# A hybrid retention / DeltaNet trunk on one core: waits for each bank apart, a weight split moved ahead of a root, small joins placed among q products, and the columns of q made at another place

## The reference, cut to what matters

```
proj = h @ w_in                                   # q | k | v | z | beta | a
q, k, v = silu(causal depthwise conv of q|k|v)
q = l2norm(q) * d**-0.5 ; k = l2norm(k)           # the norms are columns: one number per head and token
lower = strict part of (k b) k^T * decay           # 64-token chunks in the reference; tiles of 128 in the kernel
a_mat = eye + lower ; sol = triangular_solve(a_mat, [v b, k b exp(g)])
qk = q k^T * decay
scan over chunks: v_new = u - w S ; out = q_dec S + qk v_new ; S = S exp(g_last) + k_dec^T v_new
o = rmsnorm(out) * silu(z) ; out = o @ w_out
```

## Time and profile before

| | |
|---|---|
| three timed runs | 1481.12, 1483.14, 1483.98 us; median 1483.14 |
| the profiled execution | 1481.87 us, of which 1480.1 us are the span of the trace |
| TensorE busy | 1453.2 us, 98% of the span |
| TensorE weight loads | 1220.5 us, 82% |
| VectorE, ScalarE, GpSimd busy | 591.6 (40%), 546.0 (37%), 655.5 us (44%) |
| mean granted TensorE clock | 0.993 of full |
| TensorE on the chain that ended last | 90% of the span |

### The profile page before, as it was taken

How to read it: one execution, slowest core, us unless ns; L and a number is a source line. 1 busy time by engine, 2 the same in 40 slices (tenths; PEclk the granted TensorE clock), 3 DMA queues, 4 the chain that set the end, 5 groups by cost and what they waited for, 6 DMA issues and landing times.

```text
span 1480.1 us, 19872 instructions
## 1 busy us (share of the span) xinstructions
PE 1453.2 (98%) x7772; PEld 1220.5 (82%) x7773; DVE 591.6 (40%) x1095; ACT 546.0 (37%) x1039; POOL 655.5 (44%) x306
## 2 busy tenths in 40 slices
PE   8999999999999999999999999999998999999998
PEld 6988888757889888888888977889988988888886
DVE  3641001264265520044037445797756640024223
ACT  5232243254243222222225457754734322123231
POOL 6245344343544353444447216357435444434442
PEclk9999999999999999999999999999999999999999
DMA  6322322400233223323232222221113132232321
GB/s 220 127 86 85 105 93 88 165 3 29 90 111 116 86 85 103 97 85 114 86 114 86 89 87 86 86 83 35 57 57 129 58 100 99 88 110 87 106 94 57
DMA packets 66557, 136.23 MB, mean 92 GB/s; under 512 B 3632, under 2 KB 4016, under 8 KB 66096
## 3 DMA queue, kind: packets, MB, share of 16 engines
q1 hardware_dynamic: 64016, 125.90, 25.8%
q10 hardware_dynamic: 2464, 9.25, 1.7%
HBM read 133.03 MB, written 2.11 MB: 91 GB/s over the span
## 4 chain that ended last, share of the span: by engine, by line
PE 90%; DVE 4%; ACT 3%; POOL 2%; DMA 1%; issue 1%; DVEq 0%; ACTq 0%; SPq 0%; POOLq 0%
PE bank L452 27%; PE bank L453 27%; PE bank L454 27%; PE bank L660 2%; POOL side_lo L331 1%; PE bank L774 1%; PE bank L646 1%; PE bank L730 1%; POOL w_lo L331 1%; DVE mix L1610 1%; DVE gv L1837 1%; ACT squares L1351 1%; PE bank L499 1%; DVE act_lo L1652 0%; DMA gains<-in_norm_gains_dram 0%
## 5 line engine op out<-in xcount | busy, mean ns | idle before, releaser
L331 POOL TENSOR_TENSOR w_lo<-w_raw,w_hi 128x1024 fp32r<-128x1024 f32 (+1 forms) x218 | 521.5, 2415 | 679.1 <-ACT w_hi L1050 676.2
L1050 ACT ACTIVATE w_hi<-w_raw 128x1024 fp32r<-128x1024 f32 x208 | 209.1, 1055 | 467.1 <-PE bank L454 424.5
L452 PE MATMUL bank<-act_hi,w_hi 128*128 128x512 f32 (+1 forms) x816 | 295.0, 362 | 7.7 <-DVE act_lo L1652 4.4
L454 PE MATMUL bank<-act_hi,w_lo 128*128 128x512 f32 (+1 forms) x816 | 293.3, 359 | 0.0
L453 PE MATMUL bank<-act_lo,w_hi 128*128 128x512 f32 (+1 forms) x816 | 293.2, 359 | 0.0
L453 PE MATMUL bank<-w_lo,hid_hi 128*128 128x512 f32 x480 | 189.0, 394 | 0.0
L452 PE MATMUL bank<-w_hi,hid_hi 128*128 128x512 f32 x480 | 188.2, 392 | 0.0
L454 PE MATMUL bank<-w_hi,hid_lo 128*128 128x512 f32 x480 | 186.4, 388 | 0.0
L452 PEld LDWEIGHTS bank<-act_hi,w_hi 128*128 128x128 f32 x816 | 155.0, 190 | 32.6 <-DVE act_lo L1652 5.5
L1759 DVE TENSOR_TENSOR relu_sq<-relu 128x512 f32<-128x512 f32 x64 | 48.6, 759 | 329.0 <-ACT relu L1076 328.4
L454 PEld LDWEIGHTS bank<-act_hi,w_lo 128*128 128x128 f32 x816 | 155.0, 190 | 22.6
(11 more groups left out here) (280 smaller groups left out, 2169.2 us busy)
## 6 DMA issues: line engine op xcount, KB each, us to landing
w_raw<-in_mlp_w_up_dram SPq DMA_DIRECT2D x32, 1024.0 KB, 5.8
w_raw<-in_mlp_w_down_dram SPq DMA_DIRECT2D x32, 1024.0 KB, 5.0
w_raw<-in_ret_w_in_dram SPq DMA_DIRECT2D x22, 1024.0 KB, 5.1
w_raw<-in_gdn_w_in_dram SPq DMA_DIRECT2D x16, 1024.0 KB, 5.3
w_raw<-in_ret_w_out_dram SPq DMA_DIRECT2D x8, 1024.0 KB, 4.8
w_raw<-in_gdn_w_out_dram SPq DMA_DIRECT2D x4, 1024.0 KB, 5.0
gains<-in_norm_gains_dram ACTq DMA_DIRECT2D x7, 512.0 KB, 6.1
raw_side<-in_ret_w_in_dram SPq DMA_DIRECT2D x2, 1024.0 KB, 15.2
```

The source lines that it names most:

```text
L331: done = nc.gpsimd.tensor_tensor(LO[slot][:, kt, :], RAW[raw][:, kt, :], HI[slot][:, kt, :].bitcast(F32), ALU.subtract)
L452: pe.matmul(dst, sta_hi, mov_hi, start=first, stop=False)
L454: return pe.matmul(dst, sta_lo, mov_hi, start=False, stop=last)
L1050: act.activation(HI[raw if slot is None else slot][:, kt, :], RAW[raw][:, kt, :], ACT.Copy)\
```

## The change

Seven edits, all within the DeltaNet layer:

1. In `begin`, the wait for `small_out` (three small copies out of PSUM) moves from behind the transposes to behind the next half chunk, `(0, 1)`.
2. `sum_g` moves from behind part (1, 0) to behind part (1, 1) of group 0.
3. `triangles(0)` moves from behind part (0, 2) to behind part (0, 3) of group 1.
4. `drained(gi)` becomes `drained(gi, m)`: it is called before each of the four parts of the first chunk and waits for the readers of that one bank.
5. ScalarE splits the second chunk of the second v group before it waits for and takes the root for k, and not behind it.
6. The q products of heads 2 to 7 are placed between the joins: heads 2 and 3 behind `small_halves(0)`, 4 behind `small_halves(1)`, 5 behind `small_corners(0)`, 6 behind `small_corners(1)`, 7 behind `wide_half(0)`. VectorE's `scale_products` follows that order, and ScalarE seeds in two halves.
7. ScalarE takes the root for q ahead of the copies of the wide halves, and VectorE's `q_columns` moves from behind `fade_keys(0)` to between the scaling of head 6 and the scaling of head 7.

```diff
-            def group(c, parity, chunks, features_out, a_hi, a_lo, aside={}, tiles=None):
+            def group(c, parity, chunks, features_out, a_hi, a_lo, aside={}, tiles=None, ahead=None):
...
                     for m in range(4):
+                        if ahead and j == 0:
+                            ahead(m)
                         done = part(c, j, parity, chunks, m, features_out, a_hi, a_lo, fresh=m == 0)
...
-                        if within and (g, j) == (0, 0):
-                            within()
+                        if within and (g, j) in within:
+                            within[g, j]()
...
-            def drained(gi):
+            def drained(gi, m):
 
                 if gi == 1:
-                    pe.wait_ge(sem("kq_squared"), GH)
-                    pe.wait_ge(sem("g_sums_read"), 2)
-                if gi in (2, 3):
-                    pe.wait_ge(sem("triangled"), 4 * (gi - 1))
+                    pe.wait_ge(sem("kq_squared"), 4 + m + 1)
+                    if m == 3:
+                        pe.wait_ge(sem("g_sums_read"), 2)
+                if gi in (2, 3) and m % 2:
+                    pe.wait_ge(sem("triangled"), 4 * (gi - 2) + 3 + m // 2)
                 if gi == 4:
-                    pe.wait_ge(sem("v_turned_out"), GH)
+                    pe.wait_ge(sem("v_turned_out"), 4 + m + 1)
                 if gi == 5:
-                    pe.wait_ge(sem("kq_squared"), 2 * GH)
-                    pe.wait_ge(emptied, 4 * GDN_Z[0])
+                    pe.wait_ge(sem("kq_squared"), GH + 4 + m + 1)
+                    if m == 0:
+                        pe.wait_ge(emptied, 4 * GDN_Z[0])
...
+
+                def small_gone():
                     pe.wait_ge(sem("small_out"), 3)
 
-                begin(2, beta_a, small_ones)
+                begin(2, beta_a, {(0, 0): small_ones, (0, 1): small_gone})
...
-                        (GDN_V, True, {(0, 3): lambda: turn_k(0), (1, 0): sum_g, (1, 2): lambda: turn_k(4)}),
-                        (GDN_V, True, {(0, 2): lambda: triangles(0), (1, 1): lambda: triangles(2)}),
+                        (GDN_V, True, {(0, 3): lambda: turn_k(0), (1, 1): sum_g, (1, 2): lambda: turn_k(4)}),
+                        (GDN_V, True, {(0, 3): lambda: triangles(0), (1, 1): lambda: triangles(2)}),
...
-                    drained(gi)
-                    group(start[1] + 2 * p, p, 2, features_out, act_hi, act_lo, aside)
+                    group(start[1] + 2 * p, p, 2, features_out, act_hi, act_lo, aside,
+                          ahead=lambda m: drained(gi, m))
...
                 small_halves(0)
+                q_products(2, 4)
                 small_halves(1)
-                q_products(2, 6)
+                q_products(4, 5)
                 small_corners(0)
+                q_products(5, 6)
                 small_corners(1)
+                q_products(6, 7)
                 for v in range(4 * TT):
                     wide_half(0, v // (2 * TT), v % (2 * TT))
-                q_products(6, GH)
+                q_products(7, GH)
...
-                elif gi > 2:
+                elif gi > 3:
                     splits(start, p, 2, last=1)
...
                 if gi == 2:
+                    splits(GDN_V, 1, 2, last=1)
                     act.wait_ge(sem("kq_x_made"), 1)
                     act.activation(ct[:, 2, :], ct[:, 0, :], ACT.Sqrt).then_inc(sem("kq_rooted"), 1)
...
             small_halves_out(0)
+            seed(0)
             small_halves_out(1)
-            act.wait_ge(sem("inv_t_cleared"), 1)
-            for q in QUARTERS:
-                act.activation(inv_t[q, batch_units(0), q], flipped[q, batch_units(0), :], ACT.Copy)\
-                    .then_inc(sem("seeded"), 1)
+            seed(2)
             upright_join(0)
+            splits(GDN_OUT, 0, 2, last=1)
             upright_join(1)
-            splits(GDN_OUT, 0, 2, last=1)
+            act.wait_ge(sem("kq_x_made"), 2)
+            act.activation(ct[:, 3, :], ct[:, 1, :], ACT.Sqrt).then_inc(sem("kq_rooted"), 1)
             wide_halves_out(0)
             wide_halves_out(1)
-            act.wait_ge(sem("kq_x_made"), 2)
-            act.activation(ct[:, 3, :], ct[:, 1, :], ACT.Sqrt).then_inc(sem("kq_rooted"), 1)
...
-            scale_products(0, 6)
+            scale_products(0, 5)
             corner_copies(0)
+            scale_products(5, 6)
             corner_copies(1)
-            scale_products(6, GH)
+            scale_products(6, 7)
+            q_columns()
+            scale_products(7, GH)
             wide_copies(0)
             fade_keys(1)
             wide_copies(1)
             fade_keys(0)
-            q_columns()
```

More of the change, by code:

```diff
@@ L1481, in upright_join, with seed @@
                     .then_inc(sem("upright_joined"), 1)
+            def seed(first):
+                act.wait_ge(sem("inv_t_cleared"), 1)
+                for q in QUARTERS[first:first + 2]:
+                    act.activation(inv_t[q, batch_units(0), q], flipped[q, batch_units(0), :], ACT.Copy)\
+                        .then_inc(sem("seeded"), 1)
             small_halves_out(0)
+            seed(0)
             small_halves_out(1)
-            act.wait_ge(sem("inv_t_cleared"), 1)
-            for q in QUARTERS:
-                act.activation(inv_t[q, batch_units(0), q], flipped[q, batch_units(0), :], ACT.Copy)\
-                    .then_inc(sem("seeded"), 1)
+            seed(2)
             upright_join(0)
+            splits(GDN_OUT, 0, 2, last=1)
             upright_join(1)
-            splits(GDN_OUT, 0, 2, last=1)
+            act.wait_ge(sem("kq_x_made"), 2)
+            act.activation(ct[:, 3, :], ct[:, 1, :], ACT.Sqrt).then_inc(sem("kq_rooted"), 1)
             wide_halves_out(0)
             wide_halves_out(1)
-            act.wait_ge(sem("kq_x_made"), 2)
-            act.activation(ct[:, 3, :], ct[:, 1, :], ACT.Sqrt).then_inc(sem("kq_rooted"), 1)
             outs = gv[:, :, :].rearrange("p h (n e) -> p h n e", n=TT)
```

## The result

Twenty executions of the changed kernel have a median of 1486.02 us (1481.14 to 1489.27), twenty of the kernel before 1482.84 us (1480.20 to 1484.91). The ratio is 1.0021, with a 95% interval of 1.0013 to 1.0029: slower by 0.2%, about 3 us. The profiled execution of the changed kernel has a span of 1487.5 us against 1480.1; it took 1489.27 us, the longest of its twenty, so its stages show more loss than the median has.

A forecast was written before the change was run, and what follows sets the result against it. TensorE, busy nearly throughout, bounds the kernel, so only its stalls or low-clock stretches can be won. -0.8 + 2.9 = +2.1 us on 1481.87 gives 1484.0, or 1485.2 us at the level of the median; 8-in-10 range 1480.5 to 1490.5.

The forecast's parts named there:

- The hold: `q_columns` at its new place: six instructions each wait for one GpSimd multiplication of z, 1.24 us each; `turn_keys(4)` at 1024.6 us.
- The projections: Edits 1 to 5, up to the first join: small TensorE waits go, projections end 3.9 us earlier, bounds 3 and 5.
- The bound that I named for being wrong: Start of the joins: the prediction is wrong if the first joins start less than 3 us earlier than before.
- The joins: Edit 6, first join to `turn_keys(4)`: clock stays up, TensorE there 15.1 us behind the start instead of 18.9.
- the stand: TensorE's standstill before `turn_keys(4)`, waiting for the scaling of head 7: from 1017.6 to 1024.6, 7 us.
- The clock behind the wait: TensorE behind its wait before `turn_keys(4)`: clock at 0.50 for 5.8 us after the restart, 2.9 us lost.
- my slower rival: Behind the wait before `turn_keys(4)`, the clock stays down until the scan: 1488.0 to 1490.9 us; chance 28%.

The follow-up runs named there:

- the second run: The changed kernel once more, unaltered, for a second profiled execution: 1486.49 us, ratio 1.0021.
- The filler: The changed kernel with 24 extra float32 matmuls of 128 x 128, result unused, put before the wait of `turn_keys(4)`: 1482.22 us, ratio 0.9995.

## Why the prediction was right, and where its terms were off

The direction and the mechanism of the loss were right. That the number came within 0.8 us is in part luck: what comes ahead of the clock was 0.7 us better than forecast, the clock 2.8 us worse in most executions, and the rest is where the median falls.

**The hold (the step that decided): right.** I had six instructions at 1.24 us each, one for each instruction of GpSimd, the reciprocal free. Six took 0.95 to 1.20. The length follows GpSimd's (1.2 beside z, 2.27 beside the low part) and vanishes when GpSimd is held back. By the Trainium skill (SBUF — State Buffer, Who interferes with whom) the shared ports are locked for the whole instruction by whoever issues first, and a reciprocal is not among the instructions that it names as taking the lock; both agree with these rows. That only one VectorE instruction gets in per GpSimd instruction, although each of them is short, the rows show and that section does not state.

**The projections: 3.9 us said; 4.2 measured where the clock stays up, 2.6 where it does not.** L501 to the first join went from 201.33 to 197.12 in one profile of the changed kernel and to 198.76 in the other. (From the 201.8 to 202.0 of the three other profiles with the old projections it would be 4.7 to 4.9 and 3.0 to 3.2.) The heads of groups 1, 4 and 5 are free of idle time and the wait before `triangles(2)` grew to 1.9, as the prediction had it. What it lacked is that this grown wait can cost the clock, 1.6 us. The bound that I named for being wrong, joins less than 3 us earlier, was crossed in the first profile by this: 2.6 us behind L501, and 1.1 us counted from the start of the span. In the second they come 4.2 us earlier.

**The joins: 15.1 us said, 16.7 measured.** That the clock would stay up was right. But I priced the product groups by the groups of two heads at full clock; the single heads between joins start 1.09 us before what follows them, not 0.85, and that is 1 us for four of them; the other 0.6 us I have not traced. It cost the change nothing, as `turn_keys(4)` waited anyway: 21.64 us behind the first join where the prediction has 1024.6 - 1002.5 = 22.1. For the same reason, and because `turn_keys(4)` came 0.5 us sooner behind the first join than I had it, the stand was 4.9 us and not 7. The sum of these three steps, -4.2 + 2.75 = -1.5 us, is what the chains gave; I said -0.8.

**The clock behind the wait: the term that was mis-sized.** The forecast took 2.9 us; the rows give 2.0 in one kind of execution (7.70 against 5.71 us) and 5.0 + 0.7 = 5.7 in the other (10.68 and 6.70 against 5.71 and 5.96). The second is the mechanism of my slower rival. Both profiles of the changed kernel have it, and by their times and mean clocks so have most of its executions, so it sets the median. (That rival had 1488.0 to 1490.9, from a loss of 5.7 to 8.6 and only 0.8 us won ahead of it.) With it the sum is -1.5 + 5.7 = +4.2 us over the kernel before, in the other kind +0.5. The two groups of the second run stand 3.8 to 6.2 us above and 0.5 to 1.2 us below the kernel before beside them (1482.21), so the sum for the lower one is 1 to 1.7 us too high. The forecast of 1485.2 lies near the median of 1486.0 not because executions have a loss of 2.9 us there, but because the median falls at the lower edge of the upper group; that is luck. The filler shows the size by itself: with the stand filled, 3.8 us of the median come back. Two readings behind this term were weak. The prediction's "lasted 6.8 us each" leaves out the stretch of 3.4 us at 12.6 us. And it is open whether its price, half of 5.8 us at the restart, is lost there to the end: at the same restart the changed kernel has only 3.4 us of low clock and is 0.9 us ahead 40 matmul records on, but 150 records on both stand 20.9 us behind the restart.

**A page that the runs speak against.** In the run with `triangles(2)` later TensorE did nothing from 1022.95 to 1026.56 but transposes, then less than 0.9 us of joins, and the clock was up before 1027.4; with edit 7 alone it did nothing but transposes from 1032.77 to 1036.38, and the clock was up before 1036.4. In the two profiles of the changed kernel it stayed down through the same work. By the Trainium skill (TensorE: Matmul & The Clock Gate, Part 4: PE-mode transpose) transposes don't count as busy for the clock. By that rule alone the clock should have stayed down in all four, and in two it did not.

**What stays open.** Why the low stretch lasts 6.8 us in some executions and 13.6 in others. In the short one the clock fell 2.6 us before TensorE started again (1020.4 and 1022.95), in the two long ones 1.3 and 1.5 us before (1025.8 and 1027.07; 1022.4 and 1023.92). Edit 7 alone fits this: 3.2 us before (1029.6 and 1032.77), and a short one of 6.8 us. That moving `triangles(2)` shifts one against the other is only argued; four profiles are too few. My expectation for that run missed by 3 us because I had not reckoned with the two lengths at all.

## What to carry to other kernels

Before a chain of small VectorE instructions on SBUF operands is moved, look at what GpSimd is doing at the new place: each of them but the reciprocal waited out one GpSimd instruction here, so eight instructions worth 2 us became 7.8, and one wait on GpSimd's side gave it back. When a stall is taken out of the busiest engine, ask what the engine now reaches too early; a wait costs its length and can then cost the clock, as the one of 1.9 us did in half of its profiles and the one of 4.87 us in all three. And when times of one kernel spread over 8 us where its neighbour has 5, list them with their mean clock before taking the median for the effect.

## What the runs showed of the hardware that was not expected

TensorE's clock fell behind a wait of only 1.9 us, in three of the six profiles that have this wait. How long it then stays at the 1.2 GHz level is not settled by the wait: 13.6 us behind the stand of 4.87 us in two profiles, 6.8 us in one of a kernel that differs by one slot 130 us earlier, and 6.8 us behind the longer stand (7.44 us) of edit 7 alone; the times of the changed kernel suggest both lengths in one kernel, which no pair of its profiles shows. Up to the second step the two differ by 3.7 us, and in the second set of times the two groups lie 4.2 us apart at their nearest. It falls behind some 4 us of 32 x 32 joins although TensorE never stands, and does not fall when one head of 128 x 128 products stands between each two of them: so it is in all nine kernels with edit 6, while it fell in the kernel before, with edit 7 alone and with edits 1 to 5 or 1 to 4.
